# The values of a cached-attention step: which operand of the matmul stands still

## The reference, cut to what matters

```
past_v = cache_v[page_table].reshape(dec_b, past_len, N_HEADS, 2 * HEAD_DIM)
...
p = jax.nn.softmax(s, axis=-1)
w = p[:, :, 0] - lam * p[:, :, 1]
return jnp.einsum("bhqk,bkhe->bqhe", w.astype(v.dtype), v)
```

## Time and profile before

| | |
|---|---|
| time, median of 3 runs | 2901.32 us (2894.37 to 2904.08) |
| time of the profiled execution | 2895.58 us |
| its span, first to last instruction | 2893.8 us |
| PE busy / PEld busy | 2595.5 us (90%) / 2457.6 us (85%) |
| DVE / ACT / POOL busy | 1229.5 / 540.1 / 801.5 us |
| mean granted clock of TensorE | 0.942 of full speed |
| values of the samples, matmul records | 256, 30.6 us busy, 281 ns mean |

### The profile page before, as it was taken

How to read it: one execution, slowest core, us unless ns; L and a number is a source line. 1 busy time by engine, 2 the same in 40 slices (tenths; PEclk the granted TensorE clock), 3 DMA queues, 4 the chain that set the end, 5 groups by cost and what they waited for, 6 DMA issues and landing times.

```text
span 2893.8 us, 40699 instructions
## 1 busy us (share of the span) xinstructions
PE 2595.5 (90%) x16204; PEld 2457.6 (85%) x16204; DVE 1229.5 (42%) x2126; ACT 540.1 (19%) x1188; POOL 801.5 (28%) x439
## 2 busy tenths in 40 slices
PE   0368869999999999998999688888999999999997
PEld 0356669999999999998999666657999999999997
DVE  7876132343333333338105266683353333333337
ACT  2111132220000000003112155552130000000002
POOL 4163113223322233222333201130222223322230
PEclk9956579999999999999999899999999999999998
DMA  2423321111111111111232312333111111111101
GB/s 84 97 31 46 86 88 52 44 37 44 52 51 44 44 44 52 52 44 45 88 108 83 95 49 85 84 109 117 44 37 44 52 44 44 52 52 44 44 30 59
DMA packets 78887, 173.80 MB, mean 60 GB/s; under 512 B 18762, under 2 KB 41546, under 8 KB 78674
## 3 DMA queue, kind: packets, MB, share of 16 engines
q1 hardware_dynamic: 74994, 157.84, 18.8%
q10 hardware_dynamic: 3744, 13.74, 1.2%
HBM read 143.51 MB, written 25.69 MB: 58 GB/s over the span
## 4 chain that ended last, share of the span: by engine, by line
PE 83%; DVE 10%; issue 3%; DMA 2%; ACT 2%; SPq 1%; DVEq 0%; ACTq 0%
PE pair L1421 81%; DVE acc L913 2%; DVE act_lo L913 1%; DVE nmx L1289 1%; PE pair L1719 1%; DVE tmp L941 1%; DMA u<-U 1%; DVE diag L935 0%; DVE rho L1312 0%; DVE U L1081 0%; DVE wmix L1317 0%; PE pair L1683 0%; DMA vT<-vt 0%; DVE bbar L913 0%; DVE W_t L913 0%
## 5 line engine op out<-in xcount | busy, mean ns | idle before, releaser
L1421 PE MATMUL pair<-act_hi,w_hi 128*128 128x344 f32 x3264 | 1050.1, 322 | 35.8 <-DVE act_lo L913 33.5
L1421 PE MATMUL pair<-act_hi,w_lo 128*128 128x344 f32 x3264 | 1047.3, 321 | 0.0
L1421 PE MATMUL pair<-act_lo,w_hi 128*128 128x344 f32 x3264 | 1046.8, 321 | 0.0
L1421 PEld LDWEIGHTS pair<-act_hi,w_hi 128*128 128x128 f32 x3264 | 619.3, 190 | 37.2 <-DVE act_lo L913 25.1
L534 POOL CAST w_hi<-w_raw 128x1024 fp32r<-128x1024 f32 x180 | 195.8, 1088 | 1564.4 <-PE pair L1421 814.6
L1421 PEld LDWEIGHTS pair<-act_hi,w_lo 128*128 128x128 f32 x3264 | 618.2, 189 | 0.0
L1421 PEld LDWEIGHTS pair<-act_lo,w_hi 128*128 128x128 f32 x3264 | 617.2, 189 | 0.0
L537 POOL TENSOR_TENSOR w_lo<-w_raw,w_hi 128x1024 fp32r<-128x1024 f32 x180 | 434.2, 2412 | 32.5 <-POOL w_hi L534 32.5
L913 DVE TENSOR_TENSOR tmp<-gate,pair 128x344 f32<-128x344 f32 x132 | 67.7, 513 | 736.4 <-ACT gate L745 736.4
L913 DVE TENSOR_TENSOR X<-X,pair 128x344 f32<-128x344 f32 x552 | 270.3, 508 | 200.7 <-PE pair L1421 200.6
L1421 PE MATMUL pair<-hid_lo,w_hi 128*128 128x344 f32 x1056 | 338.6, 321 | 0.0
(11 more groups left out here) (222 smaller groups left out, 2131.7 us busy)
## 6 DMA issues: line engine op xcount, KB each, us to landing
w_raw<-w SPq DMA_DIRECT2D x180, 512.0 KB, 3.5
kpg<-cache_k SPq DMA_DIRECT2D x16, 512.0 KB, 9.2
vpg<-cache_v SPq DMA_DIRECT2D x16, 512.0 KB, 4.3
X<-x_t SPq DMA_DIRECT2D x3, 1376.0 KB, 10.3
vt<-stage ACTq DMA_DIRECT2D x8, 516.0 KB, 4.7
y_t<-Y SPq DMA_DIRECT2D x3, 1376.0 KB, 5.4
ublk<-u SPq DMA_DIRECT2D x32, 128.0 KB, 5.1
z<-zblk SPq DMA_DIRECT2D x32, 128.0 KB, 3.2
```

The costliest lines, as they stand in the source:

```text
L1421: return t_.matmul(out, lhsT, rhs, start=start, stop=stop)
```

## The change

The operands of the samples' values change places. The stationary operand is the page's 128 x 128 block of a head, the moving one a single column of `wtok`, and the result one column of `bank[6]`, with the head's 128 elements on the partitions. It is already in the orientation in which the next step wants it. `wpad`, `eye8` and its constant transfer, the copy to `orow`, its 8 transposes and the semaphores `d_wp`, `d_row` and `d_ot` go. TensorE starts the values when `wtok` is there (`d_wc`), and VectorE's addition waits for the last sample (`d_o`). Both pages of a sample are now waited for before its first matmul, and the two pages of a head are added in adjacent matmuls.

```
@@ VectorE
             dve.wait_ge(d_wc, 1)
-            for j in range(NPG):
-                W5 = [P, NS, NH, NS]
-                last = tt(wpad[:, j], bc(wtok[:, j, :].rearrange("p (b h) -> p b h", b=NS), 3, W5),
-                          bc(eye8[:].rearrange("p (b m) -> p b m", b=NS), 2, W5), ALU.mult)
-            last.then_inc(d_wp, 1)
             head_low(1)
...
-            dve.wait_ge(d_ot, 1)
-            c.step(tt(oS[:], oS[:], bank[6][:, 0:64].rearrange("p (h b) -> p b h", b=NS), ALU.add))
+            dve.wait_ge(d_o, NS)
+            c.step(tt(oS[:], oS[:], bank[6][:, 0:64].rearrange("p (b h) -> p b h", b=NS), ALU.add))
@@ ScalarE
-            act.wait_ge(d_o, NS)
-            a.activation(orow, pair[2][0:NS, :], ACT.Copy).then_inc(d_row, 1)
@@ TensorE, sample_values(b)
                 for j in range(NPG):
                     pe.wait_ge(vpg_in[2 * (b % 2) + j], 16 * (b // 2) + 16)
-                    for h in range(NH):
-                        last = mm(pair[2][0:NS, h * P:(h + 1) * P], wpad[:, j, b, h, :],
-                                  vpg[:, 2 * (b % 2) + j, h * P:(h + 1) * P],
-                                  b == 0 and j == 0 and h % 4 == 0, b == NS - 1 and j == NPG - 1 and h % 4 == 3)
+                for h in range(NH):
+                    at = b * NH + h
+                    for j in range(NPG):
+                        last = mm(bank[6][:, at:at + 1], vpg[:, 2 * (b % 2) + j, h * P:(h + 1) * P],
+                                  wtok[:, j, at:at + 1], j == 0, j == NPG - 1)
                 last.then_inc(d_o, 1)
...
-            pe.wait_ge(d_wp, 1)
+            pe.wait_ge(d_wc, 1)
             for b in range(NS):
                 sample_values(b)
                 if b + 2 < NH:
                     head(b + 2)
-            pe.wait_ge(d_row, 1)
-            for h in range(NH):
-                last = t_.transpose(bank[6][:, h * NS:(h + 1) * NS], orow[:, h * P:(h + 1) * P], ident[0:NS, 0:NS])
-            last.then_inc(d_ot, 1)
```

More of the change, by code:

```diff
@@ L122, in build @@
         evenodd = place("evenodd", [P, 2], F32)
-        eye8 = place("eye8", [P, 64], F32)
         ptab = place("ptab", [1, NS * NPG], I32)
@@ L239, in build @@
         qrow = place("qrow", [NS, HC, 8, 8], F32, rg)
-        orow = qrow[:].rearrange("b c m j -> b (c m j)")
-        wpad = nc.alloc_sbuf_tensor_at("wpad", [P, NPG, NS, NH, NS], F32, offset=RAW_AT + 8192)
         vpg = nc.alloc_sbuf_tensor_at("vpg", [P, 4, DM], F32, offset=MISC_AT)
@@ L291, in build @@
         op_ready, op_added = sem("op_ready"), sem("op_added")
-        d_wp, d_row, d_ot = sem("d_wp"), sem("d_row"), sem("d_ot")
         q_zero, on_r, on_p = sem("q_zero"), sem("on_r"), sem("on_p")
@@ L373, in _ @@
             const(evenodd[:], d["c_evenodd"])
-            const(eye8[:], d["c_eye8"])
             const(ptab[:], d["page_table"])
@@ L1828, in constants @@
         "c_evenodd": np.stack([p % 2 == 0, p % 2 == 1], 1).astype(f),
-        "c_eye8": np.tile(np.eye(NS, dtype=f).reshape(1, 64), (P, 1)),
         "c_cos": np.cos(ang).astype(f)[rows],
```

## The result

The changed kernel takes 2918.11 us in the median (2916.52 to 2924.05, 5 runs), the kernel before beside it 2899.8 us (2891.11 to 2904.08, 5 runs): ratio 1.0071, 95% interval 1.0049 to 1.0093. It is slower, by 18 us in the medians, and lies in the range of the forecast. The profiled execution took 2916.52 us with a span of 2914.7. A second comparison, at another time, gave 2922.26 against 2902.99 us, ratio 1.0068 (1.0051 to 1.0086).

What follows compares the result with a forecast made beforehand. All TensorE time in the values stage, and its clock, was taken to be on the path. At half clock the addition comes +26.1 us later; with -0.7 and 0.2 this sums to +25.6 on 2895.6: 2924 us taken, range 2911 to 2935.

Steps and rivals of the forecast that it cites:

- What goes off the path: Around the values stage: values start 1.3 us earlier, and copy, 8 transposes and hand-overs behind it go, 1.8 us: -3.1 us.
- The load sets the price: Value matmuls: loading 128 stationary columns costs 110 ns a record at full clock, 216 ns at half, 6.9 us a sample.
- The 216 ns: Value matmuls at half clock: a record with a 128-column load, priced from a stream of 8 in 1647.06 - 1645.33 us.
- The head at half clock: The 8 transposes of `head` between samples: 1.85 us each at half clock, where they took 1.02 us; six times.
- The clock: TensorE in the values stage: half clock from within the first sample to the end; some 29 us of the sum.
- The reading by busy time: TensorE's clock set by how busy it recently was: full clock would stay in the stage, change about -2 us.
- The first 1 us at full clock: Start of the values stage: clock still full there, giving 1 us back, stage 65.4 us instead of 66.4.
- The row that decided it: `outputs_s5`, nearest case for the stage: PE busy 30.00 of 30.00 us at clock 0.50, rising at once with hidden loads.
- The output projection: Behind the stage: finds half clock as before, which lasted 6 us or 3.1 us; 1.4 us less or the same, -0.7.
- The pages: Page transfers in the stage: 6.1 us needed, 10.6 us lie over them at half clock, so hidden.
- the rival in which the clock holds: Values stage at full clock but for 3 us, page waits 1.8 us: -1.8 us, 2899.5 us; chance 0.11.
- The sum: Whole kernel at half clock: VectorE's addition +26.1 us later, projection -0.7, `d_ssq` matmul 0.2 slower: +25.6 us.

Runs made afterwards that it cites:

- the kernel with three places for pages: Changed kernel with 64 moving columns instead of one and a third place for a sample's pages; 2892.81 us against 2896.64 for the kernel before, ratio 0.9987.
- the run with 64 columns: Changed kernel with each value matmul moving 64 columns instead of one, VectorE picking the 8 wanted; 2902.98 us, ratio 1.0024 to the kernel before.

## Why the prediction was right, step by step

- **What goes off the path, -3.1 us.** As forecast: the first value follows the copy's beginning by 0.39 us instead of 1.71, and the addition follows the last record by 0.1 us instead of 1.9. The profile after shows both.
- **The load sets the price.** Shown: 110 ns a record at full clock, 207 at half clock (6.62 / 32), and half of that with 64 stationary columns. The 216 ns that I took from the transposes at half clock were 4% too much: 2.3 us of the sum.
- **The head at half clock**, 1.85 us forecast, 1.81 measured.
- **The clock.** As forecast, and that the moving columns make the difference is shown: with 32 and 64 of them everything else that TensorE does is equal, and with 64 the clock came back inside a stream without a gap. The reading by busy time is wrong here. The first 1 us at full clock was about right too: the mean of 0.55 over the first 6.4 us makes 0.6 us.
- **The row that decided it**, the 30 us of `outputs_s5`, was read too simply, and in this the forecast had some luck. The clock did not rise at once when the matmuls with 16 stationary columns came; the earlier trace rows leave out the stretch between, which stands below: these matmuls begin at 199.77 us, and the clock is 0.50 to 204.4. And `outputs_s5` moved 6 x 136 columns in 1.95 us, 418 a microsecond, and stayed at 0.50, while the kernel with three places for pages moved 32 x 64 + 8 x 128 columns in 6.72 + 1.71 us, 364 a microsecond, and came back to 1.00. So the count of moving columns is not the whole of it. Two of three matmuls of `outputs_s5` have 64 rows and not 128; whether that is the reason no run tested, and what TensorE's clock goes by stays open.

```profile
199.77 0.61 PE L1421 MATMUL pair<-G_re,bpad 128*16 128x128 f32 x2
...
201.00:204.00 3.00, 3.00 (x16) 2.12 (x14) 0.00 (x0) 0.53 (x1) 3.00 (x2) 0.50 1.12 166
```

- **The output projection** had half clock for 4.9 us (2.8, and 2.1 of the next 3.0) and not 6, which I had put at -0.7 us; yet the part behind the addition came out 0.3 us longer than before, so this gain does not show in the whole.
- **The pages.** Hidden, as forecast. The price for the rival in which the clock holds was mis-sized: 1.8 us forecast, 4.0 to 4.8 measured when the clock is full. With it that rival comes to about nothing instead of -1.8 us: the run with 64 columns, which kept the clock, lost all of the 3.1 us in these waits.
- **The sum.** +25.6 us forecast, +24.5 in the stage, +18 and +19 in the medians, with the interval up to 27. My forecast of 2924 us stood 3 us above the profiled sum because of the runs' median; in the profiled execution the untouched attention took 3.9 us back, and why the medians lie still nearer stays open.

## What to carry to other kernels

Which operand of a matmul stands still is no free choice when one side is thin: a block of 128 columns that is used once cost its load here, 110 ns a record at full clock, whether 64 columns moved past it or, at half clock with 207 ns, one or 32. What was hidden beneath 128 moving columns becomes the price. Before turning a matmul around, look for a stretch of the same kernel where loads outweigh moving columns and read the granted clock there; busy time said nothing of it here. With a thin stationary side the gain lay in the other direction, in putting four of them beside each other in the array.

## What the runs showed of the hardware that was not expected

Four column groups brought a record of 8 stationary and 128 moving fp32 columns from 112 to 31 ns at full clock. A VectorE subtraction of 128 x 64 took 2.22 us beside a GpSimd subtraction and 0.28 without it. With 64 moving columns to 128 stationary ones the clock stood at either level in executions of one kernel, and the times scattered over 26 us.
